# Two transformer blocks on one core: the keys and values of both memory attentions are made in earlier mixers

## What is computed

```python
# first model
for i in range(2):
    h, hc = modulate(rmsnorm(x)), modulate(rmsnorm(ctx))
    y, y_c = (ab_mixer, cd_mixer)[i](h, hc)      # 2nd mixer: Fourier mix + gated linear attention
    x = x + g_m * y
    x = x + g_f * swiglu(modulate(rmsnorm(x)))   # ctx likewise, in layer 0 only
x = rmsnorm(x)
# second model
mixer_0(x)     # 3rd mixer: a score picks keys for each query (top-k), attention over them, window attention
x = layernorm(ALPHA * x + cross(x, mem, layer=0)); swiglu
mixer_1(x)     # 4th mixer: compressed, selected and window attention
x = layernorm(ALPHA * x + cross(x, mem, layer=1)); experts (8, two chosen per token)

def cross(x, mem, layer):        # memory attention, 4 heads of 128, 256 memory rows
    q, k, v = x @ w_q[layer], mem @ w_k[layer], mem @ w_v[layer]
    return softmax(q k^T / sqrt(128)) v @ w_o[layer]
```

## Time and profile before

| | |
|---|---|
| Median of 3 runs | 3076.69 us (3075.2 to 3077.16) |
| The profiled execution | 3077.61 us, of which its span is 3075.8 us |
| TensorE (PE) busy | 2766.3 us, 90% of the span |
| VectorE (DVE) busy | 1757.1 us, 57% |
| ScalarE (ACT) busy | 1128.8 us, 37% |
| Granted TensorE clock, mean | 0.94 |
| Loaded from HBM | 594.28 MB, 194 GB/s over the span |

### The profile page before, as it was taken

How to read it: one execution, slowest core, us unless ns; L and a number is a source line. 1 busy time by engine, 2 the same in 40 slices (tenths; PEclk the granted TensorE clock), 3 DMA queues, 4 the chain that set the end, 5 groups by cost and what they waited for, 6 DMA issues and landing times.

```text
span 3075.8 us, 36773 instructions
## 1 busy us (share of the span) xinstructions
PE 2766.3 (90%) x14142; PEld 2193.2 (71%) x14142; DVE 1757.1 (57%) x1944; ACT 1128.8 (37%) x1428; POOL 7.0 (0%) x15
## 2 busy tenths in 40 slices
PE   4798789999895999959899978879999999999998
PEld 0233448888654899747799856668888888888886
DVE  0101545555415677161588353278878788788887
ACT  1210410000213100141200143167777777777776
POOL 0000000000000000000000000000000000000000
PEclk7899899999996999979999988979999999999999
DMA  9543012222220555303255311249889899898995
GB/s 407 215 191 150 15 55 97 97 97 96 78 82 6 191 183 182 112 1 123 96 178 179 127 64 69 96 180 367 339 330 373 322 354 351 330 373 330 350 346 227
DMA packets 82657, 596.52 MB, mean 194 GB/s; under 512 B 9040, under 2 KB 10064, under 8 KB 11024
## 3 DMA queue, kind: packets, MB, share of 16 engines
q1 hardware_dynamic: 80960, 583.04, 50.2%
q0 software_dynamic: 1616, 12.32, 1.0%
HBM read 594.28 MB, written 1.05 MB: 194 GB/s over the span
## 4 chain that ended last, share of the span: by engine, by line
PE 84%; DVE 6%; ACT 4%; DMA 3%; issue 3%; DVEq 0%; SPq 0%; ACTq 0%; POOLq 0%
PE bank L437 15%; PE bank L607 8%; PE bank L611 8%; PE bank L610 8%; PE bank L1498 7%; PE bank L1501 7%; PE bank L1502 7%; PE bank L451 4%; PE bank L1531 3%; PE bank L1534 3%; PE bank L1535 3%; DMA ring<-in_stream 2%; ACT arena L791 2%; PE bank L467 2%; DVE arena L882 1%
## 5 line engine op out<-in xcount | busy, mean ns | idle before, releaser
L577 DVE TENSOR_TENSOR ring_part<-ring,arena_part 128x2048 fp32r<-128x2048 f32 x437 | 983.9, 2285 | 59.2 <-ACT arena_part L1767 54.8
L1767 ACT ACTIVATE arena_part<-ring 128x2048 fp32r<-128x2048 f32 x339 | 642.5, 1918 | 151.9 <-DMA ring<-in_stream 151.8
L607 PE MATMUL bank<-arena_part 128*128 128x256 f32 (+1 forms) x1584 | 510.2, 322 | 30.4 <-issue 24.4
L611 PE MATMUL bank<-arena_part,ring_part 128*128 128x256 f32 (+1 forms) x1584 | 507.1, 320 | 0.0
L1498 PE MATMUL bank<-arena_part 128*128 128x512 f32 x896 | 355.2, 396 | 3.3 <-issue 2.8
L1501 PE MATMUL bank<-ring_part,arena_part 128*128 128x512 f32 x896 | 349.8, 390 | 0.0
L1502 PE MATMUL bank<-arena_part 128*128 128x512 f32 x896 | 349.5, 390 | 0.0
L607 PEld LDWEIGHTS bank<-arena_part 128*128 128x128 f32 x1584 | 304.0, 192 | 57.8 <-issue 26.0
L610 PE MATMUL bank<-h_part,arena_part 128*128 128x256 f32 (+1 forms) x1056 | 339.1, 321 | 0.0
L437 PE MATMUL bank<-h_normed,ring 128*128 128x256 f32 (+1 forms) x1024 | 307.6, 463 | 25.4 <-issue 14.2
L611 PEld LDWEIGHTS bank<-arena_part,ring_part 128*128 128x128 f32 x1584 | 304.4, 192 | 21.0
(11 more groups left out here) (259 smaller groups left out, 3020.0 us busy)
## 6 DMA issues: line engine op xcount, KB each, us to landing
ring<-in_stream SPq DMA_DIRECT2D x555, 1024.0 KB, 4.8
consts<-in_small POOLq DMA_DIRECT2D x1, 3067.0 KB, 14.5
arena<-in_ab_bias POOLq DMA_DIRECT2D x1, 2048.0 KB, 34.1
arena<-in_t_bias POOLq DMA_DIRECT2D x1, 2048.0 KB, 9.7
x_stream<-in_x_t POOLq DMA_DIRECT2D x1, 1024.0 KB, 21.3
x_stream<-in_ctx_t POOLq DMA_DIRECT2D x1, 1024.0 KB, 27.7
x_stream<-in_mem_t POOLq DMA_DIRECT2D x1, 1024.0 KB, 5.7
arena<-in_band_bias POOLq DMA_DIRECT2D x1, 1024.0 KB, 11.7
```

The source lines that it names most:

```text
L577: return nc.vector.tensor_tensor(low, value, high.bitcast(F32), ALU.subtract)
L607: m = nc.tensor.matmul(out_ap, w_high, high, start=start, stop=False)
L611: return nc.tensor.matmul(out_ap, w_low, high, start=False, stop=stop)
L1767: nc.scalar.activation(high, ring[:, where], ACT.Copy).then_inc(sem("moe_high"), 1)
```

## The change

The six products that make keys and values from `mem` (four of `products`, two of `token_products`, named `mem_products`) leave `cross`. Those of layer 1 go into the second mixer, between the rotations and the first DFT products; those of layer 0 into the third, between the selector products and the attention. They have places of their own until they are used: layer 1 the `ctx` half of `hv`, layer 0 an area of the arena. ScalarE empties their banks (`mem_out`) in place of VectorE: behind its exponentials in the second mixer, behind the selector's in the third. POOL loads `mem` once the second mixer's input is normalised, ahead of its wait for `cd_done`. The stream's order follows, and `FFN_AT` with it.

```diff
-        xk = area(1024, 1024, "p (c t) -> p c t", c=4)
-        xvv = area(2048, 1024, "p (t e) -> p t e", t=2)
+        mem_keys = [area(10272, 1024, "p (c t) -> p c t", c=4), hv[:, 0:4, SEQ:TT]]
+        mem_values = [area(11296, 1024, "p (t e) -> p t e", t=2).rearrange("p t (j e) -> p t j e", j=2),
+                      hv[:, 4:8, SEQ:TT].rearrange("p (t j) e -> p t j e", t=2)]
...
+            def mem_products():
+
+                products(bk, w, 4, lambda k: xv[:, k, SEQ:TT], SEQ)
+                token_products(bk, w, lambda k, t: xv[:, k, SEQ + t * P:SEQ + (t + 1) * P], 2)
...
             products(bk, w, 4, h_x, SEQ, ready=h_ready(2))
+            marks["cd_normed"] = bk.count["h_ready"]
...
-            for taken in bk.all_freed(marks_f := bk.turn - 25, 4):
+            pe.wait_ge(sem("mem_landed"), 16)
+            mem_products()
+            for taken in bk.all_freed(bk.turn - 31, 4):
                 pe.wait_ge(*taken)
             for g in range(4):
...
             for taken in bk.all_freed(bk.turn - 24, 8):
                 pe.wait_ge(*taken)
+            mem_products()
             pe.wait_ge(sem("bias_landed"), 48)
             outs = attention_pe(bk, dsa_steps())
...
                 products(bk, w, 4, x_x, SEQ, ready=lambda k: pe.wait_ge(sem("ln_ready"), bk.up("ln_ready")))
-                pe.wait_ge(sem("mem_landed"), 16)
-                products(bk, w, 4, lambda k: xv[:, k, SEQ:TT], SEQ)
-                token_products(bk, w, lambda k, t: xv[:, k, SEQ + t * P:SEQ + (t + 1) * P], 2)
-                for taken in bk.all_freed(bk.turn - 10, 10):
+                for taken in bk.all_freed(bk.turn - 4, 4):
                     pe.wait_ge(*taken)
-                outs = attention_pe(bk, cross_steps())
+                outs = attention_pe(bk, cross_steps(n // 3))
...
+            def mem_out(layer):
+                for c in range(4):
+                    to(mem_keys[layer][:, c, :], cols=SEQ)
+                for t in range(2):
+                    b = bk.next_bank()
+                    act.wait_ge(full(b), bk.filled())
+                    nc.scalar.activation(mem_values[layer][:, t, :, :], PS[b][:, :].rearrange("p (j e) -> p j e", j=2),
+                                         ACT.Copy).then_inc(free(b), 1)
...
-            dft_turn = bk.turn
+            mem_out(1)
             act.wait_ge(sem("k_decayed"), 4)
...
                 to(relu_buf[n % 2], ACT.Relu, cols=SEQ, scale=64 ** -0.5)
+            mem_out(0)
             attention_act(bk, dsa_steps())
...
                 bk.turn += 4
-                for c in range(4):
-                    to(xk[:, c, :], cols=SEQ)
-                for t in range(2):
-                    to(xvv[:, t, :])
-                attention_dve(bk, cross_steps())
+                attention_dve(bk, cross_steps(n // 3))
...
+            pool.wait_ge(sem("h_ready"), marks["cd_normed"])
+            pool.dma_start(xv[:, :, SEQ:TT], mem_t.rearrange("p (c t) -> p c t", c=DC)).then_inc(sem("mem_landed"), 16)
             for taken in marks["cd_done"]:
                 pool.wait_ge(*taken)
-            pool.dma_start(xv[:, :, SEQ:TT], mem_t.rearrange("p (c t) -> p c t", c=DC)).then_inc(sem("mem_landed"), 16)
```

More of the change, by code:

```diff
@@ L67 @@
 FFN_AT = [SLOTS_ADA + 10 + 4]
-FFN_AT.append(FFN_AT[0] + SLOTS_FFN + 8 + 4)
-FFN_AT.append(FFN_AT[1] + SLOTS_FFN + 8 + 4 + 8)
+FFN_AT.append(FFN_AT[0] + SLOTS_FFN + 8 + 4 + 4)
+FFN_AT.append(FFN_AT[1] + SLOTS_FFN + 8 + 4 + 4 + 4)
 HIGH_AHEAD, LOW_AHEAD = 3, 2
@@ L1014, in band_steps, with cross_steps @@
             return steps
-        def cross_steps():
+        def cross_steps(layer):
+            xk, xvv = mem_keys[layer], mem_values[layer]
             steps = []
@@ L1025, in cross_steps @@
                         [score_buf[a % 3][:, 512 * u + P * j:512 * u + P * (j + 1)] for j in range(4)],
-                        [(PS[o][:, (2 * u + t) * P:(2 * u + t + 1) * P], xvv[:, n, h * P:(h + 1) * P],
+                        [(PS[o][:, (2 * u + t) * P:(2 * u + t + 1) * P], xvv[:, n, h // 2, h % 2 * P:(h % 2 + 1) * P],
                           probs(a, u, 2 * t + n), n == 0, n == 1) for t in range(2) for n in range(2)],
@@ L1730, in cross @@
                     to(xq[:, c, :], cols=SEQ)
-                bk.turn += 6
-                attention_act(bk, cross_steps())
+                attention_act(bk, cross_steps(n // 3))
                 bk.turn += DC
@@ L1962, in _ @@
                         .then_inc(sem("qk_ready"), 1)
-            bk.turn += 4 + 4 + 4
+            bk.turn += 6 + 4 + 4 + 4
             for d in range(2):
@@ L2068, in _ @@
                 dve.wait_ge(sem("dve_step"), bk.up("dve_step"))
+            bk.turn += 6
             dve.wait_ge(sem("bias_landed"), 48)
@@ L2476, in _layout, with mem @@
     ada = [_by_row(w[:, n:n + 2048]) for w in i["ada_w"] for n in range(0, 6 * D, 2048)]
+    def mem(l):
+        return [_by_column(i["xa_w_k_2"][l]), _by_row(i["xa_w_v_2"][l])]
     w = i["ab_w_in"][0]
@@ L2483, in _layout @@
     tiles += [_by_column(w[:, 0:1024]), _by_column(w[:, 1536:2048]), _by_row(w[:, 1024:1536])]
+    tiles += mem(1)
     tiles.append(_by_column(i["cd_w_out"][0]))
@@ L2490, in _layout @@
     tiles.append(_by_row(w[:, 1864:1992]))
+    tiles += mem(0)
     w = i["ev_w_out_2"][0]
@@ L2494, in cross @@
     def cross(l):
-        return [_by_column(i["xa_w_q_2"][l]), _by_column(i["xa_w_k_2"][l]), _by_row(i["xa_w_v_2"][l]),
-                _by_column(i["xa_w_o_2"][l])]
+        return [_by_column(i["xa_w_q_2"][l]), _by_column(i["xa_w_o_2"][l])]
     tiles += cross(0)
```

## The result

The changed kernel takes **3033.28 us** (median of 4 runs, 3030.49 to 3033.68), the kernel before beside it 3076.93 us (3075.2 to 3077.39). The ratio is 0.9857, with a 95% interval of 0.984 to 0.9874: 43.7 us, 1.4% faster. The profiled execution took 3033.36 us over a span of 3031.6. The forecast was 3034.8 (3028 to 3050), faster.

The account below looks back on a forecast made before the run. The prediction took TensorE as the bound, holding 84% of the chain that ended last. Its terms, -28.14 - 28.15 + 6.2 + 8.2 = -41.9 us, took the median 3076.7 to 3034.8 us, range 3028 to 3050.

Parts of the forecast that it names:

- The memory attentions, -28.14 and -28.15: With key and value products gone, scores wait only for the last query eviction: 28.14 and 28.15 us saved.
- The second mixer, +6.2: 27.7 us of products added behind the rotations delay the second DFT products 8.2 us; full clock returns 2.0.
- The bound of 10: Second mixer, upper bound of the added cost: 10 us if transposes and DFT run at half clock.
- The third mixer, +8.2: Products added behind the selector matmuls let VectorE take the first score at 1343.3 against 1335.12: 8.2 us later.
- The bound of 4.5: Second mixer, lower bound of the added cost: 4.5 us if the clock helps later matmuls too.
- The memory load and the weight stream, 0: POOL's earlier memory load (issued at 833.8, needed by 920.4) and eight earlier weight slots cost nothing.
- Rival 4: Memory rows land late in the second mixer; landing as late as before gives +112.8 us, 3147.6; chance 0.02.
- The sum, -41.9: Whole kernel: -28.14 - 28.15 + 6.2 + 8.2 = -41.9 us, from a median of 3076.7 to 3034.8.
- 1 (the clock): Moved products start at half clock in the third mixer, or it falls inside the attentions: +10, 3045 us; chance 0.08.
- 2 (one site hides nothing): Evictions or banks put 27.7 us after the selection (3054 us) or the scans (3056 us); chance 0.06.
- 3 (the weight stream): The end follows the weight stream, losing the second attention's gain before the experts: -13.7, 3063 us; chance 0.02.
- 5 (no effect): The wait on the scores is set elsewhere and the saving returns as idle time: 3077 us; chance 0.02.

Follow-up runs that it names:

- layer0_only: The changed kernel with layer 1's keys and values put back behind the queries of the second memory attention, layer 0's still early; 3061.0 us.
- pieces: The changed kernel with the values' products cut into two column halves, each half put into a wait of TensorE; 3019.98 us.
- keys_only: The changed kernel with both layers' value products put back behind the queries of the memory attentions, only the keys early; 3048.42 us.
- keep_busy: The changed kernel with extra fp32 matmuls, their result overwritten, in three waits of TensorE; 3032.4 us.
- values1_later_gap: The changed kernel with layer 1's value products moved to the second mixer's later gap, ahead of its output products; 3031.64 us.

## Why the prediction was right

*The memory attentions, -28.14 and -28.15:* -27.85 each. The mechanism was as stated (the scores hang on the last query eviction). The term mis-sized is the gap behind it: I took 0.06 us (and named 0.1 as the sign) and it is 0.37, close to the 0.36 that the earlier trace rows show between VectorE's last copy (1467.48 + 0.69) and the scores. The table load cost nothing. The -27.85 also holds a stretch of half clock that both kernels have in the query products; in layer0_only and pieces, which lack it, the first attention gives -29.54.

*The second mixer, +6.2:* +6.1. The steps: products at 920.98 (forecast 920.41), end at 948.5 (948.1), transposes at 951.98 (951.6) at full clock in 1.92 us (1.9), second DFT products at 954.98 (954.6), state products at 962.06 (961.6). With the 0.5 us of the later start each is met within 0.2. The bound of 10, all at half clock, did not come near: clock 1.00 through 27.50 us and on. The rule of "TensorE: Matmul & The Clock Gate", Part 1, in the Trainium skill, that activity releases the clock, agrees with these rows.

*The third mixer, +8.2:* +7.9. VectorE took the first scores at 1347.30. My 1349.5 for it carried the 6.2 of the second mixer forward whole; the trace has +4.33 at that point, since 1.31 and 1.03 had been gained on the way. That was the step that missed most. The bound of 4.5 in the second mixer ("the clock helps later matmuls too") was meant for such gains, but 6.13 - 1.31 - 1.03 = 3.79 lies below it. keys_only, with nothing sticking out and no cost, and pieces, with +1.03 for a block that is one half shorter at the selection, show the form of the cost here: what sticks out of the wait.

*The memory load and the weight stream, 0:* 834.65 against 833.8, landing in 5.7 us as before; no wait of TensorE for either. Rival 4 has no row for it. The 34.1 us that I called the slowest POOL load is not: the profile before has one of 37.3 (`in_sgu`), which still leaves over 45 us in hand.

*The sum, -41.9:* -44.2 in the profiled spans, -43.7 in the medians. The four terms come to 6.13 + 7.86 - 27.85 - 27.85 = -41.7 with their measured sizes. The rest is -3.8 in three places where I had set nothing, +0.8 behind the scores of the two memory attentions, and +0.5 at the start. The -3.8 is more than the 2 us below that I had left for the clock elsewhere; that the total came within 2.3 us of the forecast in the profiled spans owes something to luck, as the +1.3 stands against it. One of the three, -1.46, is shown to be the bank rotation: 12 more products ahead turn the latent-value products onto other banks. The forecast said "the score banks hold keys that ScalarE has long emptied", which looked at the first scores alone and not at what a number of added turns does behind them. The other two come with the moved work of the second mixer and with a shorter stretch at half clock; what moves the clock is open, and in keep_busy more work in the waits did not enlarge them.

*The rivals:* 1 (the clock), 2 (one site hides nothing), 3 (the weight stream) and 5 (no effect) are excluded by the account: each was a matter of one row in it. Of rival 1 one thing is true, half clock inside the shortened attention (query products of 15.74 us), but the kernel before had it as well. For layer0_only alone I had expected 3055.5, and there the rival "clock" seemed to win; its rows show banks and half clock together. With the banks set right, the band scores come 1.9 us and the first scores 0.9 us sooner, and some 3 us more go with stretches at half clock.

## What to carry to other kernels

Work moved into a wait costs what sticks out of it, the work less the wait: less where the clock rises by it (9.6 us stuck out in the second mixer and cost 6.1), more where it meets half clock itself (3.9 us in values1_later_gap cost 4.8). Where it is longer than the wait, cut it: the same 55.6 us of products cost 14 us as two blocks and about nothing as six pieces over four waits. Count what added products do to a rotation of banks, since a later stage with fixed banks feels it: here 1.6 us for a shift that nobody meant, though the total did not show it. And look whether an engine at half clock is waited for: behind a 0.66 us supply it isn't.

## What was not expected of the hardware

A half-clock stretch moves with the timing ahead of it, so that gains of 1.6 us are lost in it: the same 64 records of query products took 14.05 us in two of the kernels (pieces, layer0_only) and 15.74 in six others, the change among them. And at half clock the three matmuls of a chunk in the feed-forward part (0.41 us a record, one each 0.22 us) kept just up with VectorE's split, so that a clock raised from 0.77 to 1.00 over 15 us gave back nothing.
